# Prompt attention of a two-layer decoder step: the causal mask moved into the vector engine's maximum, and the transposes of odd head pairs put ahead of the projection piece

## What is computed

```python
def mla_scores(q_lat, q_pe, ckv, kpe):
    s = jnp.einsum('bqhc,bkc->bhqk', q_lat, ckv) + jnp.einsum('bqhr,bkr->bhqk', q_pe, kpe)
    return s.astype(jnp.float32) * MLA_SCALE

    def attend(args):            # in mla_prompt
        ql, qp, qpos_b = args
        s = mla_scores(ql, qp, ckv, kpe)
        s = jnp.where(kpos[None, :] <= qpos_b[:, None], s, -jnp.inf)
        p = jax.nn.softmax(s, axis=-1).astype(ckv.dtype)
        return jnp.einsum('bhqk,bkc->bqhc', p, ckv)
```

## Time and profile before

| | us |
|---|---|
| median of 3 runs | 1460.81 (1456.54 to 1463.2) |
| the profiled execution, as timed | 1455.9 |
| its span, first to last instruction | 1454.2 |
| PE busy | 1400.0 (96%) |
| DVE busy | 692.6 (48%) |
| ACT busy | 493.2 (34%) |
| prompt attention, from the first score matmul to the last product with the values | about 82 to 236 of the span |

### The profile page before, as it was taken

The page is one execution under the profiler, slowest core; times in us unless marked ns, Lnnn a source line. Parts: engine busy times, 40 slices in busy tenths (PEclk is TensorE's granted clock), DMA queues, the critical chain, the costliest instruction groups (busy, mean ns, idle before and its releaser), DMA issues.

```text
span 1454.2 us, 28923 instructions
## 1 busy us (share of the span) xinstructions
PE 1400.0 (96%) x11573; PEld 1279.8 (88%) x11573; DVE 692.6 (48%) x1122; ACT 493.2 (34%) x954; POOL 321.3 (22%) x284
## 2 busy tenths in 40 slices
PE   7999997899999999999998999999999999999997
PEld 7656665689999999999997888889999999999996
DVE  5446776536533433434356445445563343333435
ACT  5355562334422212212245334444452221221222
POOL 2220014111511503404411000001252150330531
PEclk9999999999999999999999999999999999999999
DMA  8400013232322233233214234222232323333221
GB/s 247 120 8 1 1 46 92 78 88 59 100 85 78 86 87 87 87 87 87 87 44 121 75 106 119 74 90 74 60 101 88 87 87 89 85 93 87 85 68 62
DMA packets 203905, 120.27 MB, mean 83 GB/s; under 512 B 13990, under 2 KB 199616, under 8 KB 203808
## 3 DMA queue, kind: packets, MB, share of 16 engines
q1 hardware_dynamic: 197776, 104.74, 25.2%
q0 software_dynamic: 6032, 14.17, 3.0%
HBM read 111.30 MB, written 7.59 MB: 82 GB/s over the span
## 4 chain that ended last, share of the span: by engine, by line
PE 87%; DVE 7%; ACT 3%; issue 2%; DMA 1%; SPq 0%; DVEq 0%; ACTq 0%
PE ps L1941 62%; PE ps L2003 6%; PE ps L2166 2%; PE ps L2202 1%; DVE y L1390 1%; PE ps L2149 1%; PE ps L2260 1%; PE ps L2325 1%; DVE stat L1546 1%; PE ps L2185 1%; PE ps L1965 1%; PE ps L2343 1%; PE ps L2151 1%; DVE x L1400 1%; PE ps L2497 1%
## 5 line engine op out<-in xcount | busy, mean ns | idle before, releaser
L865 ACT CAST w_hi<-w_raw 128x1024 fp32r<-128x1024 f32 x172 | 180.3, 1049 | 680.0 <-PE ps L1941 649.2
L1941 PE MATMUL ps<-act_hi,w_hi 128*128 128x280 f32 (+1 forms) x1408 | 296.8, 292 | 4.5 <-DVE vT L1737 2.9
L1941 PE MATMUL ps<-act_hi,w_lo 128*128 128x280 f32 (+1 forms) x1408 | 295.0, 291 | 0.0
L1941 PE MATMUL ps<-act_lo,w_hi 128*128 128x280 f32 (+1 forms) x1408 | 294.0, 290 | 0.0
L1356 DVE TENSOR_TENSOR w_lo<-w_raw,w_hi 128x1024 fp32r<-128x1024 f32 x172 | 255.9, 1490 | 64.5 <-ACT w_hi L865 64.4
L1941 PEld LDWEIGHTS ps<-act_hi,w_hi 128*128 128x128 f32 x1408 | 222.6, 188 | 10.5 <-issue 9.3
L1941 PEld LDWEIGHTS ps<-act_hi,w_lo 128*128 128x128 f32 x1408 | 223.7, 189 | 0.0
L1941 PEld LDWEIGHTS ps<-act_lo,w_hi 128*128 128x128 f32 x1408 | 222.5, 189 | 0.0
L1941 PE MATMUL ps<-h_hi,w_lo 128*128 128x280 f32 (+1 forms) x928 | 193.6, 290 | 0.0
L1941 PE MATMUL ps<-h_hi,w_hi 128*128 128x280 f32 (+1 forms) x928 | 192.9, 289 | 0.0
L1941 PE MATMUL ps<-h_lo,w_hi 128*128 128x280 f32 (+1 forms) x928 | 192.8, 289 | 0.0
(11 more groups left out here) (333 smaller groups left out, 1873.2 us busy)
## 6 DMA issues: line engine op xcount, KB each, us to landing
w_raw<-in_mlp_w_up_dram SPq DMA_DIRECT2D x64, 512.0 KB, 4.1
w_raw<-in_mlp_w_down_dram SPq DMA_DIRECT2D x64, 512.0 KB, 3.8
w_raw<-in_gla_w_in_dram SPq DMA_DIRECT2D x24, 512.0 KB, 3.8
pg_ckv<-in_cache_ckv_dram SPq DMA_DIRECT2D x64, 128.0 KB, 2.4
w_raw<-in_mla_w_o_dram SPq DMA_DIRECT2D x8, 512.0 KB, 4.1
sts<-in_state_gla_dram POOLq DMA_DIRECT2D x4, 1024.0 KB, 6.2
out_dram<-sts POOLq DMA_DIRECT2D x4, 1024.0 KB, 5.1
w_raw<-in_gla_w_o_dram SPq DMA_DIRECT2D x8, 512.0 KB, 3.9
```

Of the source, the lines that this page charges most:

```text
L865: nc.scalar.copy(w_hi[slot(g)][:], w_raw[raw_slot(g)][:]).then_inc(w_rounded, 1)
L1941: last = nc.tensor.matmul(out[:, h, 0:n], w[:, c, :], a[:, c, t0 + n * h:t0 + n * h + n], start=(c == 0 and k == 0), stop=(c == DC - 1 and ...
```

## The change

It has two parts. The first takes the mask out of PE: `scores` has one matmul for units 0 to 7, and `max_scores` becomes one call that reads the scores from PSUM and a mask from SBUF, writes `-(score + mask)` back over the scores in PSUM, and returns the minimum of that, which is the negated maximum. The exponential reads the tile with scale -1. The mask is now stored for 512 columns in bf16 (zero but for the last 128), packed into the constants, which grow by 128 fp32 columns; the two bf16 copies of mask and full identity on ACT go away. The second part swaps `turn_probs(n - 2)` and the piece on PE in the steps where the next pair has 8 pieces.

```diff
+def turned_first(n):
+    return piece_at(n) is not None and len(pieces(piece_at(n)[0])) == 8
...
-C_TRIL = C_TRI + P
+C_TRIL = C_TRI + 4 * P // 2
...
-            nc.scalar.copy(identb[:], ident)
-            nc.scalar.copy(trilb[:], mcst[0:64, C_TRIL:C_TRIL + META])
-            nc.scalar.copy(trib[:], mcst[:, C_TRI:C_TRI + P]).then_inc(mask_ready, 1)
+            nc.scalar.copy(identb[:], ident[0:64, 0:64])
+            nc.scalar.copy(trilb[:], mcst[0:64, C_TRIL:C_TRIL + META]).then_inc(mask_ready, 1)
...
                 nc.scalar.activation(dst, psf[0:rows, at:at + w], ACT.Exp, bias=stat[0:rows, 0, n % 4:n % 4 + 1],
-                                     accum_out=stat[0:rows, 1, n % 4:n % 4 + 1]).then_inc(exp_done, 1)
+                                     scale=-1.0 if k < 8 else 1.0, accum_out=stat[0:rows, 1, n % 4:n % 4 + 1]).then_inc(exp_done, 1)
...
-                nc.vector.tensor_reduce(stat[0:rows, 0, n % 4:n % 4 + 1], psf[0:rows, at:at + w], AX_X, ALU.max, negate=True)\
-                    .then_inc(bias_ready, 1)
+                if k < 8:
+                    causal = mcst[:, C_TRI:C_TRIL].bitcast(BF16)[:, 4 * P - w:4 * P]
+                    nc.vector.tensor_tensor_reduce(psf[:, at:at + w], psf[:, at:at + w], causal, -1.0, 1e38, ALU.add, ALU.min,
+                                                   stat[:, 0, n % 4:n % 4 + 1]).then_inc(bias_ready, 1)
...
-                    nc.tensor.matmul(ps[:, bank, 0:P * (i + 1)], qT[b][:, P * i:P * i + P], kT[:, b, 0:P * (i + 1)], start=True, stop=False)
-                    last = nc.tensor.matmul(ps[:, bank, P * i:P * i + P], identb[:], trib[:], start=False, stop=True)
+                    last = nc.tensor.matmul(ps[:, bank, 0:P * (i + 1)], qT[b][:, P * i:P * i + P], kT[:, b, 0:P * (i + 1)], start=True, stop=True)
...
                 if n < N_UNIT:
                     scores(n)
-                    if piece_at(n) is not None:
+                    if piece_at(n) is not None and not turned_first(n):
                         piece(*piece_at(n))
                 if 2 <= n < N_UNIT + 2:
                     turn_probs(n - 2)
+                if n < N_UNIT and turned_first(n):
+                    piece(*piece_at(n))
```

More of the change, by code:

```diff
@@ L237, in constants @@
     i = np.arange(P)
-    m[:, C_TRI:C_TRI + P] = np.where(i[None, :] <= i[:, None], 0.0, -1e30)
+    tri = np.zeros((P, 4 * P), np.float32)
+    tri[:, 3 * P:] = np.where(i[None, :] <= i[:, None], 0.0, -1e30)
+    m[:, C_TRI:C_TRIL] = (tri.view(np.uint32) >> 16).astype(np.uint16).view(np.float32)
     m[:, C_TRIL:C_TRIL + META] = np.where(i[None, 0:META] <= i[:, None] % 32, 0.0, -1e30)
@@ L335, in trunk @@
                 lprobT = sb_in(s2, "lprobT", [P, len(KEYS), 64])
-                identb = sb_in(s2, "identb", [P, P], BF16)
-                trib = sb_in(s2, "trib", [P, P], BF16)
+                identb = sb_in(s2, "identb", [64, 64], BF16)
                 trilb = sb_in(s2, "trilb", [64, META], BF16)
@@ L1545, in max_scores @@
                 dve.wait_ge(s_mm, n + 1)
-                nc.vector.tensor_reduce(stat[0:rows, 0, n % 4:n % 4 + 1], psf[0:rows, at:at + w], AX_X, ALU.max, negate=True)\
-                    .then_inc(bias_ready, 1)
+                if k < 8:
+                    causal = mcst[:, C_TRI:C_TRIL].bitcast(BF16)[:, 4 * P - w:4 * P]
+                    nc.vector.tensor_tensor_reduce(psf[:, at:at + w], psf[:, at:at + w], causal, -1.0, 1e38, ALU.add, ALU.min,
+                                                   stat[:, 0, n % 4:n % 4 + 1]).then_inc(bias_ready, 1)
+                else:
+                    nc.vector.tensor_reduce(stat[0:rows, 0, n % 4:n % 4 + 1], psf[0:rows, at:at + w], AX_X, ALU.max, negate=True)\
+                        .then_inc(bias_ready, 1)
             def norm_probs(n):
@@ L2173, in scores @@
                                              start=True, stop=(at == 0), tile_position=(0, 32 * hh))
-                    last = nc.tensor.matmul(ps[0:64, bank + 1, 0:META], identb[0:64, 0:64], trilb[:], start=False, stop=True)
+                    last = nc.tensor.matmul(ps[0:64, bank + 1, 0:META], identb[:], trilb[:], start=False, stop=True)
                 last.then_inc(s_mm, 1)
```

## The result

| | before | changed |
|---|---|---|
| median of 4 runs each, us | 1460.62 (1456.54 to 1463.2) | 1451.76 (1449.79 to 1452.81) |
| ratio | 1 | 0.9946, 95% interval 0.9929 to 0.9962 |
| the profiled execution, as timed | 1455.9 | 1452.8 |
| its span | 1454.2 | 1451.1 |

The changed kernel is about 8 us faster, 0.5% (8.9 us by these two medians). The forecast was 1460.1, with a range from 1453 to 1468. Over all timed executions behind this document (14 of the changed kernel, 90 of before) the means are 1452.0 and 1459.7, which is 7.7 apart (0.8 either way, by their spread).

What follows compares the result with a forecast made beforehand. PE was taken to lead mid-attention and DVE at the end; odd pairs -2.9, even pairs +1.3, pairs 0 and 7 +1.0 gave -0.7 us (-4.5 + 43d), forecast 1460.1, range 1453 to 1468.

Steps and rivals of the forecast that it cites:

- d: Extra time per unit of DVE's new call, delaying DVE's next work and the exponential: taken as 0.09 us, bounds 0 to 0.25.
- The mask's price: On PE in attention, one mask matmul costs 0.06 us, 64 of them 3.8, gained only where PE isn't waiting anyway.
- Odd pair: Pairs 1, 3 and 5 of attention: each 0.97 us shorter, in general 1.33 - 4d.
- The QR wait: In odd pairs PE waits 0.86 us for ACT before the second QR piece; the new order saves 0.73.
- What is late next is DVE, not PE: In odd pairs up to KN0, saved masks and earlier transposes only lengthen PE's wait; three new calls give back 0.27 us.
- DVE runs almost without a pause: In odd pairs after unit 2, DVE is busy from the maximum at 144.77 to that at 150.94; QN pieces wait.
- Even pair: Pairs 2, 4 and 6: each 0.42 us longer, six new calls (6d) on the DVE and ACT loop less 0.12 for masks.
- Pair 0 and pair 7: First and last pairs of attention: +0.57 us (seven calls, one mask off) and +0.42 us (six calls, two masks).
- the new call is nearly free and the loops give way: Rival, 20%: d near 0 and odd-pair PE stalls gone, -4.5 to about -7 us, clock another 2; 1454 to 1457.
- The dear second instruction: Rival, 18%: writing out the minimum on DVE makes d 0.13 to 0.25, +1 to +6 us, 1462 to 1467.
- the swap that does nothing: Rival, 6%: PE waits for norms instead of ACT, odd pairs gain only their masks, about +1.5 us, 1462.
- the halved rate: Rival, 11%: DVE's fused instruction takes twice as long per column, d = 0.42, +13.5 up to 23 us, 1474 to 1484.

## Why the prediction was wrong

The predicted 1460.1 is 8.1 above the changed kernel's mean: 1.1 in the base, 4.4 in attention and 2.6 behind it. In the prediction's own steps:

- **The base**, 1.1: the median of before was 1460.8 in three runs and the mean is 1459.7 in 90.
- **d, 3.0 of the 4.4 that attention was off.** "I take d = 0.09" is the step that failed. 43d was 3.9; the run with the call alone has 0.8, and in the new order it is 1.0. On DVE d is 0.01 to 0.02, on the way to ACT 0.06, and on the loop of even pairs 0.035 a call. The row that I took for it (a neighbour of 32 columns whose successor starts 0.11 later) is an operation with a tile of its own to go through; the read of the accumulator starts with the next instruction. The bound "0 (hidden)" was in the text, and the rows that spoke for it were cited there: the earlier trace rows show the reciprocal starting before the maximum's record ends. By the Trainium skill, "VectorE: DVE Perf Modes", section "The DRAIN you can't avoid", the next instruction waits for the pipe to empty unless it is one that isn't held, which starts earlier. Here the reciprocal starts 0.08 before the call's record ends, as in the kernel before; the prediction named only the first half of that section.
- **The mask's price, 0.06.** Right where transposes or scores follow, too small where a piece does: 0.11. The earlier trace rows show the distance to the next start, but not that the piece behind then runs longer; the cost of the mask stood in the next gap.
- **Odd pair, 0.97 forecast, 1.6 measured.** The QR wait came out as forecast (0.73 and a little: 0.77 with the order alone, 0.82 with both). "What is late next is DVE, not PE" failed. From the maximum of unit 3 to that of unit 6 the forecast gave back 3d = 0.27; measured in odd pair 3 it is 6.01 rather than 6.17, 0.16 less. "DVE runs almost without a pause" had pauses of 0.16 and 0.10 that no idle time is recorded for. In the kernel before, the maximum of unit 5 starts 0.37 behind `split_out`, and 0.26 behind its mask matmul (148.55), as the one at 144.77 does, which has a recorded wait for the mask (144.51). In the changed kernel it starts 0.21 behind `split_out`. The maximum of unit 6 (150.94) also stands 0.26 behind its mask matmul and is 0.10 later behind the piece's reading than in the changed kernel. For unit 5, before, then changed:

```profile
148.44 0.29 DVE L1562 TENSOR_TENSOR act_lo<-ps,act_hi 128x128 fp32r<-128x128 f32 x1
148.81 0.56 DVE L1546 TENSOR_REDUCE stat<-ps 128x1 f32<-128x384 f32 x1
```

```profile
145.91 0.29 DVE L1571 TENSOR_TENSOR act_lo<-ps,act_hi 128x128 fp32r<-128x128 f32 x1
146.12 0.56 DVE L1552 CUSTOM_DVE_ANT_0 ps<-ps,mcst 128x384 f32<-128x384 f32 x1
```

  PE waited for DVE there too, hidden in the same way: a piece starts 0.06 behind its mask matmul, but in odd pair 3 the first QN piece 0.21 and KN0 0.18, which is 0.27 more. The record of the mask matmul, 0.22 long, covers it:

```profile
145.86 0.22 PE L2167 MATMUL ps<-trib,identb 128*128 128x128 bf16 x1
146.07 1.21 PE L2149 MATMUL ps<-lat,wqn 128*128 128x280 f32 x4
```

  The transposes now stand in those places, which is most of what the order alone gains at units 4 and 6. Recorded idle time has only 0.2 for all QN pieces of attention:

```profile
L2149 PE MATMUL ps<-lat,wqn 128*128 128x280 f32 x56 | 16.4, 416 | 0.2 <-DVE qT L1524 0.2
```

  So PE and DVE led in turn. With the mask alone, units 4 and 6 give back some of it, as the forecast said (PE waits longer for the pieces there); with both parts they don't.
- **Even pair, +0.42 forecast, -0.08 measured.** The mechanism was right, as the new wait for the norm at the end of each even pair shows, and the run that takes `split_out` out of the loop frees 0.61. Two terms were off: 6d is 0.21 rather than 0.54, and what is left, -0.08 - 0.21, says that the masks give 0.3 ahead of the loop's last arrival rather than 0.12.
- **Pair 0 and pair 7**, +0.57 and +0.42 forecast, +0.05 and -0.01 measured: mostly d again, with 0.16 and 0.05 for the calls rather than 0.63 and 0.54.
- **Behind attention, 2.6.** The prediction carried the change of attention through to the end one to one, apart from a word about the clock in one rival. That rival ("the new call is nearly free and the loops give way", 20%, -4.5 to -7, and 2 more from the clock) is the case that came in; its range of 1454 to 1457 stopped short of adding its own parts, which give 1451.8 at the far end. Less half clock behind attention accounts for an estimated 1.6 us of it; why there is less stays open.
- **The other rivals.** The dear second instruction is out (0.8 us for all calls), and so is the swap that does nothing (4.0 us by itself). So is the halved rate: 691 ns for 512 columns against 684. By the Trainium skill, "Vector Engine (DVE) Microarchitecture Reference", section "Points that are easy to get wrong", it should not apply to a PSUM source and a bf16 one, and the trace agrees.

## What to carry to other kernels

Price an instruction by when the engine's next one starts and when its consumer starts, not by its record; the two can be 0.01 and 0.06 where the record says 0.14. A small matmul in front of a wide one can cost more than its own slot, so compare the gap behind as well. Before you call an engine that seems busy without a pause the bound, compare the starts: here waits of 0.10 to 0.16 on either side lay under the recorded length of the instruction ahead, and no idle time showed them. And where runs of one kernel spread by several us, get a second trace of it before you build a sum on the first: the one read here was 3.8 us quicker than the mean.

## What the runs showed of the hardware

- A fused add and minimum from PSUM with a bf16 operand in SBUF, writing back to PSUM, runs at the rate of a plain maximum: 431 ns against 424 for 256 columns, 691 against 684 for 512.
- Reading the accumulator is recorded with 141 ns, yet the reciprocal behind it starts only 0.01 us later and the next instruction 0.02; its consumer on ACT starts 0.06 later.
- A bf16 matmul of 128x128 ahead of an fp32 piece of 280 columns costs 0.11 us, 0.05 of it in the piece; ahead of transposes it costs 0.06.
- The same work behind attention took from 1221 to 1232 us, with 13.7 to 37.5 us of it at half clock. A delay of 4.8 us ahead of attention cost 7.1, one of 12.6 us behind attention cost 11.
